# Single-row products of zeros ahead of 22 slabs of a two-block transformer kernel, and one clearing of banks moved ahead of a slab

## Chip, cores and metric

The kernel runs on one core of a Trainium2 chip. The metric is the device time of one execution in microseconds; the time of a version is the median of its runs.

## What is computed

Two blocks on 256 tokens of width 1024, float32 throughout. The first block is a half-weighted feed-forward layer, a mixer (a short convolution and a gated delta rule), a second half-weighted feed-forward layer and a norm. The second block is a mixer of a long convolution and latent attention, and a squared-ReLU MLP. The change touches the two feed-forward layers above all:

```python
def swiglu_ffn(x, w_in, w_out):          # w_in 1024 x 5632, w_out 2816 x 1024
    gate, up = jnp.split(x @ w_in, 2, axis=-1)
    return (jax.nn.silu(gate) * up) @ w_out

h = x
h = h + 0.5 * swiglu_ffn(rmsnorm(h, ffn1_norm), ffn1_w_in, ffn1_w_out)
u = rmsnorm(h, mix_norm) @ w_mix_in      # then the mixer, from 15 column slabs of u
...
h = h + 0.5 * swiglu_ffn(rmsnorm(h, ffn2_norm), ffn2_w_in, ffn2_w_out)
return rmsnorm(h, final_norm)
# second block: z = (norm(h) * (1 + scale) + shift) @ w_in_2, column slabs again
```

## The kernel before

Every weight matrix is cut into slabs of 1 MB (128 partitions x 2048 floats) that pass through three slots. SyncE loads a slab into `raw`. ScalarE rounds it to the high part `wh`. VectorE takes the difference as the low part `wl`. TensorE then makes three products for each pair of 128x128 tiles, high x high, high x low and low x high, so that a slab is 48 pairs of a weight load and a matmul of 256 columns. A slot is free for ScalarE's next cast when TensorE's counter `taken` passes it. Only TensorE's program is changed:

- `wide` (L2006) is a slab of an input projection. It waits for the low part (`low_done`) and writes one bank of the accumulator memory. Its 48 matmuls are all line L2019.
- `deep` (L2055) is a slab of a feed-forward layer's output projection, 48 matmuls on line L2063, added into banks 0 to 3. The MLP of the second block has `deep_rows` (L2075) instead, 24 matmuls of 512 columns on line L2071.
- `clear_sums` (L2084) makes four products of zeros, one row by 512 columns, on line L2087. They zero banks 0 to 3 ahead of the sums of `deep`. The operand `zero` is one partition of 512 bf16 zeros.
- `modulate` (L2107) turns a piece of an unrelated vector, two float32 products of one column on line L2111. The trace shows each of them as two matmuls, so x4.
- `square_sums` (L2115) sums squares for a norm, four float32 products of 256 columns on line L2118. The trace shows x8.
- `ffn` (L2121) runs a feed-forward layer: a first gate slab, the norm's sums, a first up slab, then a hardware loop of 10 passes. A pass is a wait for the gate bank to be read, the next gate slab, a wait for the up bank, the next up slab, a wait for the low part of the hidden values, one `deep` slab, and `modulate`. The last output slab (L2167) stands behind the loop. In `ffn1` the banks are cleared ahead of the first up slab and four transposes (L2144) stand behind it; in `ffn2` the clearing stands behind the up slab, as the last thing ahead of the loop.
- `mix(n)` (L2203) is slab n of the mixer's input projection; slab 0 is followed by `square_sums("n2")`, and slabs 1 to 5 follow in one piece.
- In the second block the slabs of `glu` (eight, in four pairs), `lat` (three) and `gate_b` 0 follow each other (L2388 on). The first half of each glu pair goes to one bank and the second to another. GpSimd's long convolution (lines L766 to L781) starts when the first pair is evacuated.

TensorE's order is the order of its program. A wait in it holds everything behind.

Of the kernel before, what the change touches and what calls it, by code (L numbers as in the profile page):

```python
# [16 lines left out]
P = 128  # L17
# [263 lines left out]
def two_blocks(nc, a):  # L281
    with ExitStack() as ctx:
# [5 lines left out]
        def sb(name, shape, dt=F32, where=ctx):  # L288
            if name in HOMES:
                fill = (HOMES[name] - next_byte[0]) % TURN  # L290
                if fill:
                    next_byte[0] += fill
                    where.enter_context(nc.sbuf_tensor("before_" + name, [P, fill // 4], F32))
            next_byte[0] += math.prod(shape[1:]) * (2 if dt == BF16 else 4)
            return where.enter_context(nc.sbuf_tensor(name, shape, dt))
# [17 lines left out]
        zero = sb("zero", [1, 512], BF16)  # L313
# [23 lines left out]
        ps = [ctx.enter_context(nc.psum_tensor(f"ps{i}", [P, 512], F32)) for i in range(8)]  # L337
# [135 lines left out]
        def S(name):  # L473

            name = SHARED.get(name, (name, 0))[0]
            if name not in named:
                named[name] = sem("s_" + name)
            return named[name]

        def at(name, count):  # L480

            return S(name), count + SHARED.get(name, (name, 0))[1]
# [1522 lines left out]
        def _(pe):  # L2005
            def wide(s, bank, x, y, tile_ready=None, tile_base=0, slab=None, m_tiles=2, inputs=range(KT),  # L2006
                     by_tile=False, low_ready=None):

                slab = s if slab is None else slab
                pe.wait_ge(*(low_ready or (low_done, s + 1)))  # L2010
                n = KT * P * m_tiles
                h, l = (w[:, slab % SLOTS, 0:n].rearrange("p (k m) -> p k m", k=KT) for w in (wh, wl))
                order = [(m, k) for k in inputs for m in range(m_tiles)] if by_tile else \
                    [(m, k) for m in range(m_tiles) for k in inputs]
                for m, k in order:
                    if tile_ready is not None and m == 0:
                        pe.wait_ge(*at(tile_ready, tile_base(k)))
                    for j, (w, r) in enumerate(((h, x), (h, y), (l, x))):
                        mm = pe.matmul(bank[:, m * T:(m + 1) * T], w[:, k, m * P:(m + 1) * P], r[:, k, :],  # L2019
                                       start=(m == 0 and k == 0 and j == 0), stop=(k == KT - 1 and j == 2),  # L2020
                                       skip_group_check=True)
                if inputs[-1] == KT - 1:
                    mm.then_inc(taken, 1)
# [60 lines left out]
            def clear_sums():  # L2084

                for b in range(4):
                    pe.matmul(ps[b][:, :], zero[0:1, 0:P], zero[0:1, :], start=True, stop=True, skip_group_check=True)  # L2087

            def column_sums(n, src, k_tiles, out, ready, signal=True, by_pair=False):
                pe.wait_ge(*at(*ready))  # L2090
                for k in range(k_tiles):
                    if by_pair and k % 2 == 0 and k:
                        pe.wait_ge(*at(ready[0], ready[1] + k // 2))
                    mm = pe.matmul(out, ones, src(k), start=(k == 0), stop=(k == k_tiles - 1), skip_group_check=True)
                if signal:
                    mm.then_inc(S(n + "_stat"), 1)
# [18 lines left out]
            def square_sums(n):  # L2115
                for b in range(4):
                    pe.wait_ge(*at(n + "_add", b + 1))
                    mm = pe.matmul(ps[6][:, 0:T], ones, sq[:, 2 * b, :], start=(b == 0), stop=(b == 3), skip_group_check=True)  # L2118
                mm.then_inc(S(n + "_stat"), 1)

            def ffn(name, n, high, low, prev_free):  # L2121
                s0 = FIRST[name + "_gate"]
                gate_bank, up_bank = (ps[b] for b in FF_BANKS[name])
                if name == "ffn1":
                    first_slab(gate_bank)
                else:
                    wide(s0, gate_bank, high, low, n + "_xl", one, by_tile=True)
                if name == "ffn1":
                    for k in range(KT):
                        if k % 2 == 0:  # L2130
                            pe.wait_ge(*(at("n1_sq", k // 2 + 1) if k < 4 else at("n1_sq_last", k // 2 - 1)))
                        mm = pe.matmul(ps[6][:, 0:T], ones, sq[:, k, :], start=(k == 0), stop=(k == KT - 1), skip_group_check=True)
                    mm.then_inc(S("n1_stat"), 1)
                    pe.wait_ge(*at("x_in", 4))
                    clear_sums()
                    wide(s0 + 1, up_bank, high, low)
                else:
                    square_sums(n)
                if name == "ffn1":
                    pe.wait_ge(*at("n1_std", 1))  # L2140
                    pe.wait_ge(*at("vec_loaded", 16 * (N_VEC - 1)))
                    for g in range(4):
                        rows_g = STAGE_ROWS[g]
                        mm = pe.transpose(ps[6][:, g * P:g * P + rows_g], stage[0:rows_g, g, :], ident[0:rows_g, 0:rows_g])  # L2144
                    mm.then_inc(S("vec_turned"), 1)
                if prev_free:
                    pe.wait_ge(*at(*prev_free))
                if name == "ffn2":
                    wide(s0 + 1, up_bank, high, low)
                    clear_sums()  # L2150
                with pe.Fori(0, FF_STEPS - 1) as i:
                    s = s0 + 2
                    pe.wait_ge(*at(name + "_gate", i + 1))
                    wide(i * 3 + s, gate_bank, high, low, slab=s)
                    pe.wait_ge(*at(name + "_up", i + 1))
                    wide(i * 3 + (s + 1), up_bank, high, low, slab=s + 1)
                    pe.wait_ge(*at(name + "_fl", i + 1))
                    deep(i * 3 + (s + 2), slab=s + 2)
                    modulate(i + (0 if name == "ffn1" else FF_STEPS - 1))
                pe.wait_ge(*at(name + "_fl", FF_STEPS))  # L2160
                s = s0 + 3 * FF_STEPS - 1
                pe.wait_ge(low_done, s + 1)
                h, l = (w[:, s % SLOTS, :].rearrange("p (k m) -> p k m", k=2) for w in (wh, wl))
                for m in range(KT):
                    for k in range(2):
                        for w, r in ((h, last_high[name]), (h, last_low[name]), (l, last_high[name])):
                            mm = pe.matmul(ps[m // 2][:, (m % 2) * T:(m % 2 + 1) * T], w[:, k, m * P:(m + 1) * P], r[:, k, :],  # L2167
                                           start=False, stop=False, skip_group_check=True)
                    if m in (1, 3, 5):
                        mm.then_inc(S(name + "_bank"), 1)  # L2170
                mm.then_inc(taken, 1)
# [35 lines left out]

            mix(0, tile_ready="n2_xl", tile_base=one, by_tile=True)
            square_sums("n2")
            for n in range(1, 6):  # L2210
                mix(n)

# [115 lines left out]
            for h in range(HEADS):  # L2328
                mm = pe.matmul(unit(ps[1], h), unit(k_be, h), unit(tt_mat, HEADS + h), start=(h == 0), stop=True,
                               skip_group_check=True)  # L2330
# [11 lines left out]
            for h in range(HEADS):  # L2342
                pe.matmul(unit(ps[1], h), unit(tt_mat, HEADS + h), unit(v_beta, HEADS + h), start=(h == 0), stop=False,
                          skip_group_check=True)
# [4 lines left out]
            for h in range(HEADS):  # L2349
                pe.matmul(unit(ps[2], h), unit(state, h), q_n[:, h, CH:2 * CH], start=(h == 0), stop=False, skip_group_check=True)  # L2350
                mm = pe.matmul(unit(ps[2], h), unit(v_new, HEADS + h), unit(at_mat, HEADS + h), start=False, stop=True,
                               skip_group_check=True)
# [35 lines left out]
            for n in range(4):  # L2388
                s = FIRST["glu"] + 2 * n
                if n >= 2:  # L2390
                    pe.wait_ge(*at("glu", n - 1))
                wide(s, ps[4 + 2 * (n % 2)], xh, xl, "h_xl" if n == 0 else None, one, by_tile=(n == 0))
                if n == 1:
                    pe.wait_ge(*at("f_kept", 1))
                wide(s + 1, ps[5 + 2 * (n % 2)], xh, xl)
# [22 lines left out]
            for n in range(3):  # L2418
# [5 lines left out]
                for m in range(4):  # L2424
                    for k in range(3):
                        if n == 0 and m == 0:
                            pe.wait_ge(*at("lat_yl", k + 1))
                        for j, (w, r) in enumerate(((h, yh), (h, yl), (l, yh))):
                            mm = pe.matmul(ps[QUERY_BANKS[n][m // 2]][:, (m % 2) * T:(m % 2 + 1) * T], w[:, k, m * P:(m + 1) * P],  # L2429
                                           r[:, k, :], start=(m % 2 == 0 and k == 0 and j == 0), stop=(k == 2 and j == 2),  # L2430
                                           skip_group_check=True)
# [8 lines left out]
            for m in range(NH):  # L2440
                for k in range(2):
                    for j, (w, r) in enumerate(((h, yh), (h, yl), (l, yh))):
                        mm = pe.matmul(ps[KEY_BANKS[m // 2]][:, (m % 2) * T:(m % 2 + 1) * T], w[:, k, m * P:(m + 1) * P],
                                       r[:, 3 + k, :], start=(m % 2 == 0 and k == 0 and j == 0), stop=(k == 1 and j == 2),
                                       skip_group_check=True)
# [8 lines left out]
            for b, bank in enumerate(VALUE_BANKS):  # L2454
# [3 lines left out]
                for k in range(2):  # L2458
                    for j, (w, r) in enumerate(((h, yh), (h, yl), (l, yh))):
                        mm = pe.matmul(ps[bank][:, :], r[:, 3 + k, tk * P:(tk + 1) * P], w[:, k, half * 512:(half + 1) * 512],  # L2460
                                       start=(k == 0 and j == 0), stop=(k == 1 and j == 2), skip_group_check=True)
# [42 lines left out]
            for h in range(NH):  # L2504
# [3 lines left out]
                if h % 2 == 0:  # L2508
                    n = h // 4 + 1
# [98 lines left out]
            for k in range(ADA_MLP * SLOTS + 1, MLP_STEPS):  # L2608
# [3 lines left out]
                if k == MLP_STEPS - 1:  # L2612
                    pe.wait_ge(*at("gate_ready", 1))
                    for t in range(KT):
                        mm = pe.matmul(ps[5 + t // 4][:, (t % 4) * P:(t % 4 + 1) * P], mods[:, 3, t:t + 1].to_broadcast([P, P]), ident,
                                       start=(t % 4 == 0), stop=True, skip_group_check=True)
# [3 lines left out]
                    for tk in range(2):  # L2620
                        mm = pe.matmul(ps[7][:, T + tk:T + tk + 1], z_eps[:, tk * P:(tk + 1) * P], ones[:, 0:1], start=(tk == 0),
                                       stop=True, skip_group_check=True)
# [33 lines left out]
```

## Time and profile before

| | |
|---|---|
| runs | 1014.54, 1014.75, 1016.36 us; median 1014.75 |
| profiled execution | 1016.84 us, with a span of 1015.0 us from first to last instruction |
| TensorE busy | 994.7 us, 98% of the span, 7777 matmuls |
| VectorE, ScalarE, GpSimd busy | 795.4, 502.6, 505.8 us |
| mean granted TensorE clock | 0.994 |
| matmuls of L2019 | 5,064 of 7,777 |

A matmul's row has a modelled duration that overlaps its neighbours, so what a slab costs is read from the distance between starts, or from the pieces of the chain that ended last: a piece runs from the end of what stood before it to its own last end, and 48 matmuls of 256 columns in one piece divide into a spacing.

### The profile page before, as it was taken

To read this page: it belongs to the slowest core of one execution; us is meant where nothing else is said; L and a number is where in the kernel's file an instruction comes from. 1 tells how busy PE (TensorE), PEld (TensorE's weight loads), DVE (VectorE), ACT (ScalarE), POOL (GpSimd) and SP (SyncE) were. 2 spreads that over 40 slices of the span, in tenths; PEclk is the share of its full clock that TensorE was granted. 3 is DMA by queue.
4 is the path that set the end of the run, shared out by engine and by line. 5 is a ranking of instruction groups with operands and counts; after the bars stand their busy time and mean duration, and the time that the engine had idled before them with its cause. 6 is when DMAs were issued, how large, how long until landed. Compare 5 with 4: busy or idle time off the path is not lost.

```text
span 1015.0 us, 19068 instructions
## 1 busy us (share of the span) xinstructions
PE 994.7 (98%) x7777; PEld 950.4 (94%) x7777; DVE 795.4 (78%) x801; ACT 502.6 (50%) x590; POOL 505.8 (50%) x294
## 2 busy tenths in 40 slices
PE   9999999999999999999999999999989999999997
PEld 7999999998999999999999999988979979999986
DVE  5877777699985579878777869998978887778764
ACT  7443433477532464444343766667657463434432
POOL 4676757510043017557677789998950104224400
PEclk9999999999999999999999999999989999999999
DMA  8968677646340266677677366482226627676641
GB/s 269 333 211 277 215 261 235 214 135 192 90 160 1 83 209 213 215 263 233 231 256 247 89 214 179 113 248 84 84 83 199 191 68 249 209 243 209 209 164 42
DMA packets 165997, 188.33 MB, mean 186 GB/s; under 512 B 10574, under 2 KB 155548, under 8 KB 165820
## 3 DMA queue, kind: packets, MB, share of 16 engines
q1 hardware_dynamic: 165580, 186.13, 56.9%
q0 software_dynamic: 192, 1.36, 0.4%
q8 instruction: 35, 0.57, 0.2%
q10 hardware_dynamic: 176, 0.15, 0.1%
q14 instruction: 14, 0.11, 0.0%
HBM read 186.58 MB, written 1.05 MB: 185 GB/s over the span
## 4 chain that ended last, share of the span: by engine, by line
PE 79%; DVE 11%; POOL 4%; ACT 3%; issue 2%; DMA 0%; ACTq 0%; DVEq 0%; POOLq 0%
PE ps L2019 47%; PE ps L2063 11%; PE ps L2071 9%; DVE wl L1304 3%; PE ps L2296 2%; POOL work L781 2%; DVE ps L1696 2%; POOL con L778 2%; PE ps L2242 2%; PE ps L2167 1%; ACT wh L812 1%; PE ps L2111 1%; POOL work L774 1%; PE ps L2429 1%; PE ps L2460 1%
## 5 line engine op out<-in xcount | busy, mean ns | idle before, releaser
L2019 PE MATMUL ps<-xh,wh 128*128 128x256 f32 x1208 | 341.1, 282 | 3.5 <-DVE xl L1653 1.0
L2019 PE MATMUL ps<-xl,wh 128*128 128x256 f32 x1208 | 336.8, 279 | 0.0
L2019 PE MATMUL ps<-xh,wl 128*128 128x256 f32 x1208 | 336.8, 279 | 0.0
L1309 DVE TENSOR_TENSOR wl<-raw,wh 128x2048 fp32r<-128x2048 f32 x78 | 245.6, 3149 | 59.6 <-ACT wh L818 59.6
L2019 PEld LDWEIGHTS ps<-xh,wh 128*128 128x128 f32 x1208 | 227.7, 189 | 7.8 <-issue 5.1
L2019 PEld LDWEIGHTS ps<-xl,wh 128*128 128x128 f32 x1208 | 228.0, 189 | 0.5
L2019 PEld LDWEIGHTS ps<-xh,wl 128*128 128x128 f32 x1208 | 227.4, 188 | 0.0
L818 ACT ACTIVATE wh<-raw 128x2048 fp32r<-128x2048 f32 x78 | 149.4, 1917 | 136.8 <-PE ps L2019 136.8
L1304 DVE TENSOR_TENSOR wl<-raw,wh 128x2048 fp32r<-128x2048 f32 (+1 forms) x72 | 178.5, 2486 | 33.2 <-ACT wh L812 32.5
L672 POOL TENSOR_TENSOR ada_raw<-ada_raw,c_act 128x2048 f32<-128x2048 f32 x24 | 90.1, 3755 | 206.4 <-DMA ada_raw<-in_w_ada 201.3
L812 ACT ACTIVATE wh<-raw 128x2048 fp32r<-128x2048 f32 (+1 forms) x74 | 139.3, 1887 | 60.4 <-PE ps L2019 45.9
L2019 PE MATMUL ps<-yh,wh 128*128 128x256 f32 x480 | 136.9, 285 | 1.2 <-DVE work L1824 0.7
L2019 PE MATMUL ps<-yl,wh 128*128 128x256 f32 x480 | 134.9, 281 | 0.0
L2019 PE MATMUL ps<-yh,wl 128*128 128x256 f32 x480 | 134.8, 281 | 0.0
L675 POOL TENSOR_TENSOR ada_raw<-ada_raw 128x1024 f32<-128x1024 f32 x24 | 97.6, 4069 | 1.9
L2019 PEld LDWEIGHTS ps<-yh,wh 128*128 128x128 f32 x480 | 90.9, 189 | 2.7 <-DVE work L1824 1.4
L2019 PEld LDWEIGHTS ps<-yl,wh 128*128 128x128 f32 x480 | 91.7, 191 | 0.1
L2019 PEld LDWEIGHTS ps<-yh,wl 128*128 128x128 f32 x480 | 91.4, 190 | 0.0
L2063 PE MATMUL ps<-fh,wh 128*128 128x256 f32 x320 | 89.8, 280 | 0.0
L2063 PE MATMUL ps<-fl,wh 128*128 128x256 f32 x320 | 89.8, 280 | 0.0
L2063 PE MATMUL ps<-fh,wl 128*128 128x256 f32 x320 | 89.8, 280 | 0.0
L705 POOL TENSOR_TENSOR work<-work 128x256 f32<-128x256 f32 x13 | 12.9, 995 | 126.8 <-ACT work L835 68.5
(415 smaller groups left out, 1847.6 us busy)
## 6 DMA issues: line engine op xcount, KB each, us to landing
raw<-in_ffn_w_in SPq DMA_DIRECT2D x43, 1024.0 KB, 7.3
ada_raw<-in_w_ada SPq DMA_DIRECT2D x24, 1024.0 KB, 5.0
raw<-in_ffn_w_out SPq DMA_DIRECT2D x22, 1024.0 KB, 4.9
raw<-in_w_in SPq DMA_DIRECT2D x18, 1024.0 KB, 5.4
raw<-in_w_mlp_in SPq DMA_DIRECT2D x16, 1024.0 KB, 5.6
raw<-in_w_mlp_out SPq DMA_DIRECT2D x16, 1024.0 KB, 4.9
raw<-in_w_mix_in SPq DMA_DIRECT2D x14, 1024.0 KB, 5.3
raw<-in_w_mix_out SPq DMA_DIRECT2D x4, 1024.0 KB, 5.1
```

The lines of the kernel that those rows point to most:

```text
L672: pool.tensor_tensor(ada_raw[:, :, :], ada_raw[:, :, :], c_act[:, :].unsqueeze(2).to_broadcast([P, KT, 256]), ALU.mult).then_inc(S("ada_pa ...
L675: pool.tensor_tensor(flat[:, 0:1024], flat[:, 0:1024], flat[:, 1024:2048], ALU.add).then_inc(S("ada_part"), 1)
L778: ins = pool.tensor_scalar(tap_own[:, n, :], upad[:, t, k:k + T], tap(k, t), 0.0, ALU.mult, ALU.add)
L781: ins = pool.tensor_tensor(sums, sums, tap_own, ALU.add)
L812: act.activation(wh[:, s % SLOTS, 0:n], raw[:, s % SLOTS, 0:n], ACT.Copy).then_inc(high_done, 1)
L818: act.activation(wh[:, s % SLOTS, :], raw[:, s % SLOTS, :], ACT.Copy).then_inc(high_done, 1)
L1304: dve.tensor_tensor(wl[:, s % SLOTS, 0:n], raw[:, s % SLOTS, 0:n], wh[:, s % SLOTS, 0:n].bitcast(F32), ALU.subtract).then_inc(low_done, 1)
L1309: dve.tensor_tensor(wl[:, s % SLOTS, :], raw[:, s % SLOTS, :], wh[:, s % SLOTS, :].bitcast(F32), ALU.subtract).then_inc(low_done, 1)
L1696: ins = dve.scalar_tensor_tensor(dst, upad[:, t, k:k + T], tap(k, t), conv_sum(t), ALU.mult, ALU.add)
L2019: mm = pe.matmul(bank[:, m * T:(m + 1) * T], w[:, k, m * P:(m + 1) * P], r[:, k, :], start=(m == 0 and k == 0 and j == 0), stop=(k == KT - ...
L2063: mm = pe.matmul(ps[m // 2][:, (m % 2) * T:(m % 2 + 1) * T], w[:, k, m * P:(m + 1) * P], r[:, k, :], start=False, stop=False, skip_group_c ...
L2071: mm = pe.matmul(ps[n][:, :], r[:, k, tk * P:(tk + 1) * P], w[:, k, half * 512:(half + 1) * 512], start=False, stop=stop, skip_group_check ...
```

## The change

It adds a helper, `long_zeros(bank)`, which makes one product of zeros, one row by 512 columns, into a whole bank. It is called in four places: in every pass of both feed-forward loops ahead of the gate slab, behind the wait for the gate bank and into that bank (20 executions); once ahead of the mixer's slabs 1 to 5 (into bank 5); and once between the first and the second slab of `glu` (into bank 5). In each case the slab that follows starts its own sum in that bank, so the zeros are overwritten. In `ffn2` the four clearing products move from behind the first up slab to ahead of it.

```diff
+            def long_zeros(bank):
+
+                pe.matmul(bank[:, :], zero[0:1, 0:P], zero[0:1, :], start=True, stop=True, skip_group_check=True)
+
...
                 if name == "ffn2":
+                    clear_sums()
                     wide(s0 + 1, up_bank, high, low)
-                    clear_sums()
                 with pe.Fori(0, FF_STEPS - 1) as i:
                     s = s0 + 2
                     pe.wait_ge(*at(name + "_gate", i + 1))
+                    long_zeros(gate_bank)
                     wide(i * 3 + s, gate_bank, high, low, slab=s)
                     pe.wait_ge(*at(name + "_up", i + 1))
                     wide(i * 3 + (s + 1), up_bank, high, low, slab=s + 1)
...
             mix(0, tile_ready="n2_xl", tile_base=one, by_tile=True)
             square_sums("n2")
+            long_zeros(ps[5])
             for n in range(1, 6):
                 mix(n)
...
                 wide(s, ps[4 + 2 * (n % 2)], xh, xl, "h_xl" if n == 0 else None, one, by_tile=(n == 0))
+                if n == 0:
+                    long_zeros(ps[5])
                 if n == 1:
                     pe.wait_ge(*at("f_kept", 1))
                 wide(s + 1, ps[5 + 2 * (n % 2)], xh, xl)
```

On TensorE, at the start of `ffn2`, the program before has the norm's sums (into bank 6), then the first up slab (into bank 4):

```order
L2019 MATMUL ps5<-yh,wl 128x256
L2118 MATMUL ps6<-work1,con 128x256 x4
L2019 MATMUL ps4<-yh,wh 128x256
L2019 MATMUL ps4<-yl,wh 128x256
L2019 MATMUL ps4<-yh,wl 128x256
```

and behind that slab the four clearing products, the loop's entry and the first gate slab of the loop (into bank 5):

```order
L2019 MATMUL ps4<-yh,wl 128x256
L2087 MATMUL ps0<-zero 128x512
L2087 MATMUL ps1<-zero 128x512
L2087 MATMUL ps2<-zero 128x512
L2087 MATMUL ps3<-zero 128x512
L2151 UNCONDITIONAL_BRANCH
L2151 ISA
L2010 ISA
L2019 MATMUL ps5<-yh,wh 128x256
L2019 MATMUL ps5<-yl,wh 128x256
```

In the changed program the same place reads, with its lines numbered four or five higher, the norm's sums, the clearing products and then the up slab:

```order
L2019 MATMUL ps5<-yh,wl 128x256
L2122 MATMUL ps6<-work1,con 128x256 x4
L2087 MATMUL ps0<-zero 128x512
L2087 MATMUL ps1<-zero 128x512
L2087 MATMUL ps2<-zero 128x512
L2087 MATMUL ps3<-zero 128x512
L2019 MATMUL ps4<-yh,wh 128x256
L2019 MATMUL ps4<-yl,wh 128x256
```

and behind the up slab the loop's entry, with the new product as the first matmul of the pass:

```order
L2019 MATMUL ps4<-yh,wl 128x256
L2155 UNCONDITIONAL_BRANCH
L2155 ISA
L2091 MATMUL ps5<-zero 128x512
L2010 ISA
L2019 MATMUL ps5<-yh,wh 128x256
L2019 MATMUL ps5<-yl,wh 128x256
```

So the four clearing products have moved past one slab, and a single one has taken their place in front of the first gate slab. From the second pass on, the new product has the four matmuls of `modulate` (into bank 7) in front of it. Nothing moves on the other engines.

## Rows read from the trace of the kernel before

**Rows 1.** The page: busy time, and the granted clock in 40 slices

```profile
PE 994.7 (98%) x7777; PEld 950.4 (94%) x7777; DVE 795.4 (78%) x801; ACT 502.6 (50%) x590; POOL 505.8 (50%) x294
...
PEclk9999999999999999999999999999989999999999
```

**Rows 2.** Chain that ended last, ffn1: start us, us, what

```profile
20.19 0.96 PE ps L2087 x4
21.15 5.66 PE ps L2019 x48
...
27.20 10.89 PE ps L2019 x96
38.09 5.44 PE ps L2063 x48
43.53 0.34 PE ps L2111 x4
43.87 11.41 PE ps L2019 x96
55.29 5.65 PE ps L2063 x48
```

**Rows 3.** The same chain at the start of ffn2

```profile
379.89 5.65 PE ps L2019 x48
385.55 0.96 PE ps L2087 x4
386.51 11.10 PE ps L2019 x96
397.61 5.44 PE ps L2063 x48
...
403.39 11.42 PE ps L2019 x96
414.81 5.65 PE ps L2063 x48
```

**Rows 4.** The same chain: mixer slabs 1 to 5, start of glu

```profile
213.67 28.28 PE ps L2019 x240
...
572.88 34.27 PE ps L2019 x288
```

**Rows 5.** The same chain elsewhere: behind L2218, and in the MLP

```profile
325.88 1.82 PE ps L2218 x8
327.70 5.85 PE ps L2019 x48
...
868.17 0.34 PE ps L2111 x4
868.51 5.57 PE ps L2019 x48
```

**Rows 6.** Timeline of TensorE, ffn1: start us, us, engine, line, what

```profile
43.37 0.50 PE L2111 MATMUL ps<-con,ada_sum 128*128 128x1 f32 x4
43.73 0.36 PE L2019 MATMUL ps<-xh,wh 128*128 128x256 f32 x1
43.94 0.28 PE L2019 MATMUL ps<-xl,wh 128*128 128x256 f32 x1
```

**Rows 7.** Timeline of TensorE around the four clearing products of ffn2

```profile
385.27 0.28 PE L2019 MATMUL ps<-yh,wl 128*128 128x256 f32 x1
385.48 1.03 PE L2087 MATMUL ps<-zero 1*128 1x512 bf16 x4
386.44 0.39 PE L2019 MATMUL ps<-yh,wh 128*128 128x256 f32 x1
386.66 0.28 PE L2019 MATMUL ps<-yl,wh 128*128 128x256 f32 x1
```

**Rows 8.** Stretches: us, busy us of each engine (instructions), clock, DMA share

```profile
43.40:200.00 156.60, 156.60 (x1334) 156.60 (x1333) 116.72 (x64) 61.92 (x46) 108.65 (x36) 1.00 0.73 241
213.70:241.90 28.20, 28.20 (x241) 28.07 (x241) 27.03 (x39) 19.67 (x25) 0.00 (x0) 1.00 0.66 188
577.40:640.80 63.40, 63.40 (x540) 63.40 (x540) 51.48 (x57) 40.74 (x51) 53.15 (x42) 1.00 0.60 174
641.00:664.00 23.00, 21.81 (x181) 21.29 (x179) 22.79 (x22) 15.18 (x24) 21.88 (x19) 1.00 0.52 128
```

**Rows 9.** Waits of GpSimd, then TensorE: total us, times, longest

```profile
POOL work L766 <- DVE work L1709: 7.0, 1, 7.0
POOL work L774 <- ACT hid L1053: 2.3, 1, 2.3
...
PE ps L2540 <- DVE work L1813: 2.7, 1, 2.7
```

## The prediction

> **What bounds the kernel now.** I read the page first. TensorE is busy 98% of the span and the clock is at full speed, 2.4 GHz, in nearly every slice [rows 1]. In the loop passes behind the first of `ffn1` TensorE is busy all of 156.6 us, while VectorE has 116.72, ScalarE 61.92 and GpSimd 108.65 [rows 8]. TensorE's own waits are few and lie elsewhere, the longest being 2.7 us at L2540 [rows 9]. So in the loops a nanosecond put in front of TensorE costs one and a nanosecond taken out gains one, as long as the others keep up.
>
> Then I read the chain of waits, because it lets one divide. The same 48 matmuls of `deep` take 5.44 us in the first pass of `ffn1` and 5.65 in the second [rows 2]: 113.3 ns from start to start, against 117.7. In `ffn2` it is the same, 5.44 in the first pass and 5.65 in the second [rows 3]. Shape, clock and operands are alike. The two input slabs of a pass show it too: 10.89 and 11.10 us in first passes, 11.41 and 11.42 in the next [rows 2, 3]. So there are two spacings, 4.4 ns apart, and a stream keeps the one it has: 240 matmuls of the mixer take 28.28 us (117.8 ns) and the first 288 of `glu` 34.27 (119.0 with the entry) with no change in between [rows 4].
>
> What stands ahead tells which. The wide spacing begins behind the L2111 products [rows 2, 3]. The narrow one is there behind the four clearing products, in both feed-forward layers. In `ffn2` the slab just ahead of the clearing ran at the wide one (5.65 us for 48) and the slab behind it at the narrow one. This is the reading on which my forecast rests: a 512-column product of zeros puts the stream that follows into the narrow spacing, and L2111 puts it back. What in the array makes the difference no row shows.
>
> **The change, part by part.**
>
> The new product itself. The trace has no single one, only four in a row. In steady state each adds 0.22 us. The entry and the exit cost more: from the last matmul ahead (385.27) to the second behind (386.66) are 1.39 us [rows 7]. Less three further products (0.65) and the two ordinary steps (0.24), one product in the middle of a slab stream would cost 0.50. Behind L2111 it is cheaper, since an entry is paid there already. The last zero product starts its successor 0.07 us ahead of its modelled end (386.51 against 386.44), and the zeros start 0.07 us ahead of the end of what stands before (385.55 against 385.48) [rows 7]. L2111 ends at 43.87 [rows 6], so a zero product would start near 43.80 and, by the distance from the last zero to the next matmul (0.30), the gate slab near 44.10 instead of 43.73. In pieces of the chain, which go from end to end, the zero product adds 0.31 us. Bounds: 0.24, if it can start right behind the last of the four small matmuls, and 0.50, the price in mid-stream. I take 0.31.
>
> The Trainium skill (TensorE: Matmul & The Clock Gate, "Back-to-back issue gap") gives one gap for a warm matmul, N/2.4 + 2.5 ns, which is 109 ns for 256 columns. The trace shows 113.3 and 117.7 instead. By that rule the spacing depends on columns alone and no product ahead could shorten it; the sum would then be only the cost of the new products, which is the time of the second rival below.
>
> A pass, from the second on. Behind a zero product the two input slabs take 11.10 us, as behind the clearing of `ffn2`, instead of 11.42, and `deep` 5.44 instead of 5.65 [rows 3]. That is 0.53 less, against 0.31 more: 0.22 gained a pass. Nine such passes in each layer make 18, so 4.0 us (with the bounds of the product's price, 0.5 to 5.2). The last output slab (L2167) stands behind L2111 with no zeros ahead of it and stays wide.
>
> The first passes. In `ffn1` the stream behind the transposes is narrow already, so the product only costs: 0.31, and 0.21 more because an entry behind zeros is longer (11.10 against 10.89) [rows 2, 3]: 0.5 lost. In `ffn2` the clearing moves ahead of the up slab. A slab behind a clearing takes 5.66 us [rows 2] and the one behind the norm's sums now 5.65 [rows 3]: the narrow spacing only pays for the entry. The clearing costs 0.96 on either side, and the new product then adds 0.31. So 0.3 lost.
>
> The mixer. The product costs 0.31. Slabs 1 to 5 then take 5.66 and four times 5.44, 27.42 us instead of 28.28 [rows 2, 4]: 0.55 gained on TensorE. VectorE is busy 27.03 of 28.20 us in this stretch [rows 8], so it has 1.2 us in hand over five slabs, and I book 0.45 (bounds 0.1 and 0.55).
>
> `glu`. The product stands between two slabs that follow without a gap: 0.31. The eleven slabs behind the first then take 5.66 + 10 x 5.44 = 60.06 us instead of 11 x 5.65 = 62.15, so TensorE would be 1.8 us ahead at about 640.8. Will it arrive at the end? Against it: from 641 to 664 VectorE is busy 22.79 of 23.00 us [rows 8], and GpSimd's long convolution starts only when VectorE has evacuated the first pair of slabs (it waits 7.0 us for L1709, then has one later wait of 2.3 for a scaled tap) [rows 9]. The first pair comes 0.31 later and gains only about 0.2 in its second slab, so that start does not move forward. For it: VectorE is busy only 51.48 of 63.40 us up to 640.8 [rows 8] and can follow TensorE, and GpSimd's 2.3 us wait is for ScalarE, which would come earlier. Bounds: 0.3 lost (convolution a little later, nothing else arrives) and 1.8 gained. I take half, 0.9 gained.
>
> Sum: -4.0 + 0.5 + 0.3 - 0.45 - 0.9 = -4.55 us. The profiled execution, 1016.84 us with a span of 1015.0, becomes 1012.3 with a span near 1010.5; that execution is 2.1 us over the median, which I carry over, so the forecast is 1014.75 - 4.6 = 1010.2. Nothing here is hidden under other work; if VectorE's cover in the mixer and after `glu` is gone, those two terms fall away and 1011.6 stands. With the end values of all terms the narrow-everywhere case runs from 1007.9 (-5.2 + 0.4 + 0.2 - 0.55 - 1.8) to 1015.7 (-0.5 + 0.7 + 0.5 - 0.1 + 0.3), and 1008.2 to 1012.5 holds most of it.
>
> **The rivals.**
>
> *Half of it (12%).* One product may not do what four do, or only in some passes. For: L2218, eight float32 matmuls in 1.82 us, left the slab behind it at 5.85, wide with a long entry [rows 5], so a longish interruption does not always reset the stream; and in the MLP a slab right behind the same L2111 products takes 5.57 us, narrow with an entry [rows 5], so what stands ahead of L2111 counts too. The state has more inputs than I can name. If 9 of 18 passes turn narrow: -9 x 0.22 + 9 x 0.31 = +0.8, the first passes +0.8, mixer and `glu` -1.35: +0.25, near 1015.0.
>
> *No narrow spacing at all (12%), slower.* One mechanism: a single product is too short to move the stream, and its price is paid every time on an engine with no slack. 18 x 0.31 = 5.6, first passes +0.8, mixer and `glu` +0.6: +7.0, near 1021.8. It decides when fewer than about nine passes turn. For: no row shows a lone product, and the skill's rule has only one gap. Against: each of the clearings in the two layers is followed by narrow matmuls, behind transposes and slabs alike [rows 2, 3], and what is next to the stream is the last zero product, the same one way or the other.
>
> *More than that (6%).* The narrow state survives L2111 where the pass before was narrow, so that L2167 and the mixer's slab 0 are narrow as well, and all of `glu`'s 1.8 arrives: 1008.5 or below. Against: the first pass of each layer was narrow and L2111 ended it [rows 2, 3].
>
> **How the numbers follow.** Narrow everywhere has 70%, at 1010.2; about 0.2% (2 us) is what a measurement of this kernel can tell. It is faster by more than that in 65 of its 70, and the largest rival adds 6. The half case falls within 0.2% for the most part (10 of 12), the rest beyond on the slow side; with the 5 of 70, "same" has 15. The slower rival has 12 and 2 from the half case. The range from 1007.0 to 1016.5 holds the first case nearly whole, most of the half case and part of the largest; it leaves out the slower rival. The likeliest case's own range is 1008.2 to 1012.5.
>
> **What the new profile would show.** One L2091 row ahead of each gate slab. Right: `deep` pieces of 5.44 in every pass, pairs of input slabs near 11.10, a pass of about 17.2 us instead of 17.4; the mixer's 240 matmuls near 27.4; no new TensorE waits in the loops. Wrong: `deep` at 5.65 behind a lone product, or at 5.44 only in alternate passes; a zero product that costs 0.5 or more; waits of TensorE for `wl` in the mixer; the time gained by 640.8 given back at L2429 or L2540.

## The result, and the profile after

The changed kernel takes 1020.25 us (median of 10 runs, 1017.99 to 1023.3) against 1015.91 us for the kernel before on the same chip (10 runs, 1014.53 to 1019.62). The ratio is 1.0039, with a 95% interval of 1.0025 to 1.0053: slower by 0.4%, where I had forecast 0.45% faster. The profiled execution took 1019.87 us with a span of 1018.1, 3.1 us more than before.

The page first, with the row that answers to [rows 1]: TensorE's busy time and share, then the other engines.

```profile
PE 996.0 (98%) x7799; PEld 945.4 (93%) x7799; DVE 804.8 (79%) x801; ACT 503.3 (49%) x590; POOL 506.0 (50%) x294
...
PEclk9999999999999999999999999999989999999999
```

The 22 new products are there, the clock is as it was, and TensorE still has 98% of the span: its busy time grew by 1.3 us, the span by 3.1. Where the time went has to be read from the chain. In the new line numbers the product of zeros is L2091, `modulate` L2115, `square_sums` L2122 and the last output slab L2172. The chain that ended last, in `ffn1` (start us, us, what), beside [rows 2]:

```profile
20.18 0.96 PE ps L2087 x4
21.14 5.66 PE ps L2019 x48
26.80 0.39 PE ps L2148 x4
27.19 0.32 PE ps L2091
27.51 11.10 PE ps L2019 x96
38.61 5.44 PE ps L2063 x48
44.05 0.34 PE ps L2115 x4
44.38 0.32 PE ps L2091
44.70 11.10 PE ps L2019 x96
...
61.90 11.10 PE ps L2019 x96
```

Up to here all is as forecast. A pass is 17.19 us (from 27.51 to 44.70, and to 61.90), against 17.41 before, in all ten passes. The product costs 0.31 to 0.32. The mixer, beside [rows 4]:

```profile
212.27 0.32 PE ps L2091
212.59 27.45 PE ps L2019 x240
```

27.45 us for the five slabs, where 27.42 was forecast and 28.28 stood before. The start of `ffn2`, beside [rows 3]:

```profile
376.09 1.73 PE ps L2122 x8
377.82 0.96 PE ps L2087 x4
378.79 5.66 PE ps L2019 x48
384.44 0.32 PE ps L2091
384.76 11.51 PE ps L2019 x96
396.26 5.65 PE ps L2063 x48
401.92 0.34 PE ps L2115 x4
402.25 0.32 PE ps L2091
402.57 11.50 PE ps L2019 x96
```

Here it goes wrong. The up slab behind the clearing is narrow, 5.66 as costed. Behind the lone product come 11.51 and 5.65, the wide spacing, and it stays for all ten passes. A pass is now 17.81 us: 0.40 more than before and 0.62 more than the 17.19 that I had put in. The timeline of TensorE shows the entry (start us, modelled us):

```profile
384.05 0.28 PE L2019 MATMUL ps<-yl,wh 128*128 128x256 f32 x1
384.16 0.28 PE L2019 MATMUL ps<-yh,wl 128*128 128x256 f32 x1
384.37 0.39 PE L2091 MATMUL ps<-zero 1*128 1x512 bf16 x1
384.69 0.39 PE L2019 MATMUL ps<-yh,wh 128*128 128x256 f32 x1
384.91 0.28 PE L2019 MATMUL ps<-yl,wh 128*128 128x256 f32 x1
385.03 0.28 PE L2019 MATMUL ps<-yh,wl 128*128 128x256 f32 x1
...
385.97 0.28 PE L2019 MATMUL ps<-yl,wh 128*128 128x256 f32 x1
```

From 385.03 to 385.97 are eight steps of 117.5 ns. Ahead of the product the steps were 0.11 us.

Then `glu`, beside the second line of [rows 4], and the first 288 matmuls after the long convolution:

```profile
575.38 6.07 PE ps L2019 x48
581.46 0.32 PE ps L2091
581.77 27.43 PE ps L2019 x240
...
772.57 34.87 PE ps L2019 x288
```

The `glu` slabs behind the product are narrow in this execution; the slab ahead of it was wide (its last four steps take 0.47 us, 580.71 to 581.18). The piece at 772.57 is 1.10 us longer than its counterpart before (33.77 at 770.39), and nothing was changed near it.

Put side by side, the starts of the same pieces give the account of the 3.1 us, after less before: mixer slabs 1 to 5, 212.59 against 213.67, -1.08; the last twelve matmuls ahead of the norm's sums of `ffn2`, 374.41 against 376.53, -2.12; first input slabs of its loop, 384.76 against 386.51, -1.75; start of `glu`, 575.38 against 572.88, +2.50; the piece behind the long convolution, 772.57 against 770.39, +2.18; its end +3.3; the last instruction +3.1. So `ffn2`'s passes alone lose 4.25 us. That is the first pass, 0.62 longer since it was narrow before, and nine times 0.40.

### The profile page after: what moved, and what is told of

It reads as the page before. It is cut to its first block, busy times and chain, and to the rows that moved or that the text cites. A ratio compares the mean times of both kernels' runs of the same rounds, so it can differ in the third digit from the quotient of the medians.

```text
span 1018.1 us, 19111 instructions
## 1 busy us (share of the span) xinstructions
PE 996.0 (98%) x7799; PEld 945.4 (93%) x7799; DVE 804.8 (79%) x801; ACT 503.3 (49%) x590; POOL 506.0 (50%) x294
## 3 DMA queue, kind: packets, MB, share of 16 engines
HBM read 186.58 MB, written 1.05 MB: 184 GB/s over the span
## 4 chain that ended last, share of the span: by engine, by line
PE 80%; DVE 11%; POOL 4%; issue 2%; ACT 2%; DMA 0%; ACTq 0%; DVEq 0%; POOLq 0%
PE ps L2019 47%; PE ps L2063 11%; PE ps L2071 9%; DVE wl L1304 3%; PE ps L2302 2%; POOL work L781 2%; DVE ps L1696 2%; POOL con L778 2%; PE ps L2248 2%; PE ps L2172 1%; ACT wh L812 1%; PE ps L2115 1%; PE ps L2091 1%; POOL work L774 1%; PE ps L2030 1%
## 5 line engine op out<-in xcount | busy, mean ns | idle before, releaser
L675 POOL TENSOR_TENSOR ada_raw<-ada_raw 128x1024 f32<-128x1024 f32 x24 | 87.9, 3664 | 1.9
```

What stands on the lines that cost most here:

```text
L675: pool.tensor_tensor(flat[:, 0:1024], flat[:, 0:1024], flat[:, 1024:2048], ALU.add).then_inc(S("ada_part"), 1)
```

## The experiments

The narrow spacing was there behind a lone product in `ffn1` and not in `ffn2`. My theory on reading this ("history"): a lone product doesn't set the spacing, it changes it according to what stands directly ahead. In `ffn1` four transposes stand between the up slab and the first product, in `ffn2` a narrow slab does. The rivals were the accumulator bank (the two layers use banks 4 and 5 crosswise), the buffer slot of the slab, and chance. The ratios below are against the kernel before on the same chip, with 95% intervals. A time without a number of runs is that of a single, profiled execution: what counts there is the spacing, and the time is only a guide.

**The changed kernel once more.** No edit.

> The changed kernel once more, to see whether the spacing of each place is a property of the program or of the execution. Place theory (something in the program of ffn2, bank, slot or operand, makes a lone zero product fail there): all ten passes of ffn1 narrow again (deep 5.44 us), all ten of ffn2 wide again (5.65 us, input slabs 11.50). Chance theory: in another execution the passes of ffn2 come out narrow, or those of ffn1 wide, and the time moves by up to 5 us.

1020.59 us. All ten passes of `ffn1` are narrow again and all ten of `ffn2` wide, so this is no chance. `glu` differs from the first execution. Its chain:

```profile
574.28 6.03 PE ps L2019 x48
580.32 0.32 PE ps L2091
580.63 28.48 PE ps L2019 x240
```

Wide, 1.05 us more than 27.43. The slab ahead was narrow here (its last three steps take 0.34 us, 579.70 to 580.04), the same picture as in `ffn2`, and the reverse of the first execution's `glu`. The other profiles agree. Of twelve executions with one product there (these two and ten of the versions below), the slab ahead was wide in six, and the stream behind the product narrow; in the other six it was the other way round. So the spacing of the first slab changes from one execution to the next, and the product exchanged it every time.

**Banks exchanged.**

```diff
-FF_BANKS = {"ffn1": (4, 5), "ffn2": (5, 4)}
+FF_BANKS = {"ffn1": (5, 4), "ffn2": (4, 5)}
```

> The changed kernel with the gate and up banks exchanged in both layers: ffn1 now has its gate slab and zero product in bank 5, ffn2 in bank 4. Bank theory (a lone zero product into bank 5 leaves the stream wide in a loop): ffn1 turns wide (deep 5.65 us) and ffn2 narrow (5.44 us), ffn1 about 5 us longer and ffn2 about 6 us shorter. Slot or operand theory: nothing moves, ffn1 5.44 and ffn2 5.65.

1021.06 us, and no spacing moves: `ffn1` narrow, `ffn2` wide (11.50 and 5.65 from 385.40 on). The bank theory falls.

**Every slab one slot on.** In all places alike:

```diff
-                h, l = (w[:, slab % SLOTS, 0:n].rearrange("p (k m) -> p k m", k=KT) for w in (wh, wl))
+                h, l = (w[:, (slab + SHIFT) % SLOTS, 0:n].rearrange("p (k m) -> p k m", k=KT) for w in (wh, wl))
```

> The changed kernel with every slab one slot further in memory: the gate slab of ffn1 lies in slot 0 instead of 2, that of ffn2 in slot 1 instead of 0. Slot theory (weights in slot 0 behind a lone zero product go wide): ffn1 turns wide (deep 5.65 us), ffn2 narrow (5.44 us). Bank or operand theory: nothing moves.

1020.52 us, again with `ffn1` narrow and `ffn2` wide. The slot theory falls too.

**No part of the change in `ffn2`.** The clearing stands behind the up slab and the loop has no product; the rest of the change stays.

```diff
-                    clear_sums()
                     wide(s0 + 1, up_bank, high, low)
+                    clear_sums()
...
-                    long_zeros(gate_bank)
+                    if name == "ffn1":
+                        long_zeros(gate_bank)
```

> The changed kernel with ffn2 as in the kernel before: no zero product in its loop, clearing behind the up slab. The zeros of ffn1, the mixer and glu stay. Theory that the loss is in ffn2 alone: ffn2 is back to 17.41 us a pass (its first narrow), and against the kernel before 9 x 0.21 - 0.5 in ffn1 and 0.5 to 1 in the mixer remain, about 2 us faster than the kernel before, near 1014, if the second block does not change. Rival (the second block loses by itself, since its long stretch of 252 matmuls came out wide in the changed kernel): within 1 us of the kernel before.

1014.59 us (10 runs) against 1016.09; ratio 0.9991, interval 0.9976 to 1.0006. `ffn2` is as before, a first pass of 11.10 and 5.44 and then 11.41 and 5.65. Against the change whole (1.0039) this is 0.5% better, so the loss is in `ffn2`, as the account says. The gain of 2 us that I expected to be left is not shown: the interval includes 1, and the rival, a second block that loses by itself, isn't excluded. In this execution both of its long stretches were wide (28.48 us for `glu` behind the product, 34.88 for the 288 matmuls).

**Only the clearing put back, zeros kept in every pass.**

```diff
-                    clear_sums()
                     wide(s0 + 1, up_bank, high, low)
+                    clear_sums()
```

> The changed kernel with one part undone: in ffn2 the four clearing products stand behind the up slab again, so the loop's first zero product has them, and no narrow slab, right ahead of it. History theory (what stands ahead of the first pass sets the spacing, a lone product right behind a narrow slab turns the stream wide, and the pair L2111 plus zero product hands the state of one pass to the next): all ten passes of ffn2 are narrow, deep 5.44 us and input slabs 11.10, a pass 17.19 us instead of 17.81; ffn2 6.2 us shorter than in the changed kernel, the time near 1013.5, 2 us faster than the kernel before. Layer theory (something in ffn2, its operands or its place, makes lone products fail there): the passes stay at 17.81 us and the time near 1020.

1014.84 us (10 runs) against 1017.04; ratio 0.9977, interval 0.996 to 0.9994. The chain at the start of `ffn2`:

```profile
382.78 0.96 PE ps L2087 x4
383.74 0.22 PE ps L2091
383.96 11.09 PE ps L2019 x96
395.05 5.44 PE ps L2063 x48
...
401.15 11.10 PE ps L2019 x96
```

All ten passes narrow, 17.19 us each. The loop is that of the changed kernel; only four products in front of it were moved. Its first product now ends a row of five, and the slab ahead of that row is wide (117.7 ns) as in the kernel before. So the passes of `ffn2` carry what the loop's entry gave them, through nine further lone products and through `modulate`. The price of the move is 0.62 us ten times over. I had costed it at nothing.

**A narrow slab directly ahead of `ffn1`'s first product.** The transposes go ahead of the clearing and the up slab, so that they no longer stand between that slab and the loop.

```diff
+                if name == "ffn1":
+                    clear_sums()
+                    wide(s0 + 1, up_bank, high, low)
```

> The changed kernel with the four transposes and clearing of ffn1 in another order: transposes, clearing, up slab, loop. So the narrow up slab stands right ahead of the loop's first zero product, as in ffn2. History theory: now ffn1 is wide in all ten passes (deep 5.65 us, a pass 17.81) and ffn2 stays as it is, about 6 us slower than the changed kernel. Layer theory: ffn1 stays narrow (5.44 us).

1035.13 us. About 8 us of it is a loss at the start that has nothing to do with the question: the transposes now wait 6.8 us for a load, the up slab behind them takes 7.75 us at a granted clock of 0.73 (from 28 to 36 us), and the loop starts at 36.01 instead of 27.51. The last 14 steps of that slab are narrow, 113 ns. The loop itself answers the question:

```profile
35.69 0.32 PE ps L2091
36.01 11.51 PE ps L2019 x96
47.52 5.65 PE ps L2063 x48
```

`ffn1`, narrow in every version seen up to here with zeros, is now wide in all ten passes. What stands directly ahead of the first product decides for either layer.

**A lone product ahead of every slab of the mixer's five and of `glu`.** `long_zeros` goes into `mix` and into both halves of the pairs.

> The changed kernel with a zero product ahead of each of the mixer's slabs 1 to 5 and of each of the seven glu slabs behind the first, instead of one. Flip theory (a lone product right behind a stream exchanges the spacing): slabs alternate, about 5.65 and 5.44 us for 48 matmuls without the entry, from slab to slab. Reset theory (it gives narrow behind wide and wide behind narrow only by its timing there, or always one of them): all slabs behind a product look the same after the second. Time beyond the changed kernel: 10 x 0.5 = 5 us at most.

1024.41 us. The chain in the mixer:

```profile
212.53 5.67 PE ps L2019 x48
...
218.52 5.85 PE ps L2019 x48
...
224.69 5.66 PE ps L2019 x48
...
230.66 5.85 PE ps L2019 x48
...
236.83 5.67 PE ps L2019 x48
```

With its entry, a slab is 5.66 us narrow and 5.85 wide. They alternate strictly, here and through the seven `glu` slabs behind a product (5.85, 5.66, 5.85, 5.66, 5.85, 5.66, 5.87). Directly behind a slab, then, a lone product exchanges the spacing: narrow becomes wide, and wide narrow. Had I had this row, the forecast for `ffn2` would have been wide.

**Two, three and four products a pass.** The same call written two, three or four times ahead of the gate slab. A new question arose from the last run: if one exchanges, do two leave it alone (parity), or does a longer row set the narrow one (reset)?

> The changed kernel with two zero products in each pass of both loops instead of one. Flip theory (parity counts): behind the narrow slab of ffn2 two products leave it narrow, and ffn2 comes out other than now in at least its first pass. Length theory (a row of products resets to narrow, a lone one does not): all passes of both layers narrow, 17.19 + 0.22 = 17.41 us a pass. If both fail, ffn2 stays wide at 18.03 us a pass.

1022.43 us. Passes alternate in both layers; `ffn2`:

```profile
388.49 0.53 PE ps L2091 x2
389.02 11.08 PE ps L2019 x96
400.11 5.44 PE ps L2063 x48
...
406.42 11.50 PE ps L2019 x96
417.92 5.65 PE ps L2063 x48
```

Two directly behind the narrow up slab leave it narrow (11.08), as two exchanges would. Two behind `modulate` exchange: narrow, wide, narrow, wide. One behind `modulate` hands on what it finds, narrow in `ffn1` and wide in `ffn2` above. `modulate` alone left wide behind either (the passes of the kernel before). I have no count that fits all three.

> The changed kernel with three zero products in each pass. With one, a pass hands on its spacing; with two, passes alternated. Parity theory (each zero product exchanges the spacing once, L2111 once more): three act as one, ffn1 narrow in all passes from the second on, or all wide, no alternation, about 17.62 or 18.24 us a pass. Reset theory (the row becomes long enough): all passes of both layers narrow.

1020.47 us, all 20 passes narrow; `ffn2`'s first behind the narrow up slab is 11.09 us. Parity wants this one wide. Directly behind a slab it holds for one and two and fails at three.

> The changed kernel with four zero products in each pass, as many as the clearing has. Parity theory: four act as two, the passes alternate between 11.08 and 11.50 us for the input slabs. Reset theory, which the three clearings seen so far suggest (narrow behind them each time, behind a wide slab as behind a narrow one): all twenty passes narrow, 17.84 us each.

1024.75 us, all 20 passes narrow (11.10, then 11.09, and 5.44). A row of three or four ends narrow wherever it was tried. But in these runs the stream ahead was always narrow. That a longer row also turns a wide stream narrow is seen only at the entry of `ffn2`: four in [rows 3] and again in the version without zeros there, five in the one with the clearing back. For three it wasn't tried. It doesn't pay: a pass is 17.61 us with three and 17.83 with four, against 17.41 with none.

**The product behind `modulate`, and four in `glu`.** With the clearing back, the lone product becomes the last matmul of the pass, so that it also stands ahead of L2172.

```diff
-                    long_zeros(gate_bank)
...
                     modulate(i + (0 if name == "ffn1" else FF_STEPS - 1))
+                    long_zeros(ps[6])
...
-                    long_zeros(ps[5])
+                    for _ in range(4):
+                        long_zeros(ps[5])
```

> A version meant to be faster: clearing of ffn2 back behind its up slab, the loop's lone zero product as the last matmul of a pass (behind L2111, into bank 6) instead of the first, and four zero products instead of one between the first two slabs of glu. Then the first passes pay for no product and the last output slab stands behind one. If the handing-on rule holds: all twenty passes narrow at 17.19 us, L2167 narrow (5.65 becomes 5.44 with a longer entry), 0.3 to 0.5 us a layer less than with the product in front; glu narrow for 11 slabs whatever its first slab was, 0.65 dearer. Against clearing_back: 0 to 1 us faster. Rival: the product's new place breaks the handing-on and the passes come out wide, then near 1020.

1014.98 us (11 runs) against 1017.41; ratio 0.9977, interval 0.9964 to 0.999. L2172 is narrow with an entry (5.66, against 5.76), all passes are narrow, and so is `glu` behind its four products (27.43, the slab ahead narrow too). It is not faster than the version with the clearing back (1014.27 beside it, below), where I had expected up to 1 us. The reset by four, though, is no rule. In this execution `ffn1`'s up slab came out wide behind its clearing, which has the norm's sums ahead of it and no slab:

```profile
18.78 0.96 PE ps L2087 x4
19.74 5.86 PE ps L2019 x48
```

The two slabs behind the four transposes were narrow all the same (10.90 us), as they are in [rows 2] behind a narrow slab. So, as far as these traces go, the transposes end narrow behind either, and the loop of `ffn1` was entered narrow.

**The version with the clearing back, once more.** No new edit, for its interval.

> clearing_back once more beside zeros_behind_modulate, for its time on the same chip and to see whether its spacings repeat: all passes narrow again, 2 us faster than the kernel before.

1014.27 us (11 runs) against 1017.41; ratio 0.9978, interval 0.9964 to 0.9991. All 20 feed-forward passes are narrow again. The 288 matmuls behind the long convolution took 34.88 us here and 33.76 in the first execution of the same kernel, so that stretch changes by itself. The two versions with the clearing back have the lowest ratios, 0.22 to 0.23% ahead of the kernel before; the version without zeros in `ffn2` (0.9991) overlaps with them.

## Why the prediction was wrong

**Price of one product: right.** 0.31 forecast, 0.31 to 0.32 measured as a piece of the chain behind `modulate`, behind L2122 and between two slabs. Between two slabs the longer entry of the next one comes on top (5.66 against 5.44), so the whole price there is about 0.5: from the last matmul ahead (384.16) to the second behind (384.91) are 0.75 us, less two ordinary steps 0.51. The 0.50 worked out for mid-stream was right too.

**`ffn1` and the mixer: right.** The nine passes gained 0.22 each and the first lost 0.5, as worked out. The mixer came to 27.45 against 27.42, and its lead arrived: -1.08 at the start of its slabs, of which the product had taken 0.31, and -1.93 at 255.65 (257.58 before). Twelve matmuls ahead of the sums of `ffn2` the changed kernel led by 2.12 us; the terms booked up to there add to 1.95.

**The failed step: "a 512-column product of zeros puts the stream that follows into the narrow spacing, and L2111 puts it back".** Every clearing that I had read was four products in a row, and I put one in. The experiments show what stands in its place. One product exchanges the spacing when it stands directly behind a slab. `modulate` alone makes the next pass wide; with one product it hands the spacing on, with two it exchanges it, and with three or four a narrow stream stayed narrow. That is why `ffn1` came out right for a wrong reason, by luck: its loop was entered narrow behind the transposes, and one product behind `modulate` hands on what it finds.

**"The clearing costs 0.96 on either side": the sum was right, the side effect missed.** The move took away the four products that made the entry narrow, and left a narrow slab directly ahead of a lone one. Forecast for the passes of `ffn2` behind that entry, -2.0; measured +4.25. This is 6.2 of the 7.6 us between the span that was forecast for the profiled execution (1010.5) and the measured one (1018.1). The other 1.4 is mostly the stretch at 772.57 (1.1) and `glu` (0.6, below).

**`glu`: the product exchanges there too, and what it finds changes.** Narrow behind it (27.43) in one execution, wide (28.48) in the next. The forecast took the first slab to be wide, as in the one trace I had; it was so in six of twelve. Where the slabs behind were narrow, little arrived in the changed kernel: the lag fell from 2.50 to 2.18 us, a gain of 0.3 for the 0.9 booked. That is inside the bounds of 0.3 lost and 1.8 gained. In the first execution with the clearing back 1.4 arrived (from -4.33 at 568.55 to -5.68 at 764.71). Over all profiles, from the start of `glu` to the piece behind the long convolution are 197.51 us before, 196.15 to 197.65 in the six executions with the one product that were narrow behind it, and 197.48 to 199.89 in the five that were wide. So, against the one trace of before, the product mostly gains in the first case and mostly loses in the second, and the 0.9 could not be booked. It isn't the spacing alone: with four products it took 200.17, and the slabs were narrow.

**The rivals.** "Half of it" had the mechanism nearest to the truth, "one product may not do what four do", and even the count: ten passes narrow, ten wide. I put it at 1015.0, and 12 in 100, since I charged a wide pass 0.31. It costs 0.40, because a wide entry behind a product is 11.50 instead of 11.42, and there are ten of them in a row, the first of which had been narrow. "No narrow spacing at all", 1021.8, is close to the measured time by accident: its mechanism is refuted by `ffn1`. The formula that I had weighed (the Trainium skill, TensorE: Matmul & The Clock Gate, "Back-to-back issue gap") is given there for an isolated matmul. For streams of weight loads and matmuls the same section has one measured spacing for 128 columns and one for 512, and none for 256. I should have said so. Neither knows a second spacing at one number of columns, and the traces have two, 113.3 and 117.7 ns by the pieces of 5.44 and 5.65.

**A slip in the sum.** The lower end of the narrow-everywhere case is 1007.8 by its own terms, not 1007.9; nothing hangs on it.

**What stays open.** What in TensorE keeps and exchanges the spacing; no row shows it. Also open is why three products do not exchange where one does, and why four did not set the narrow spacing once. Bank and slot are ruled out; whether it is the number of products or the length of the interruption that counts was not tried apart. With all passes narrow, the forecast of 0.45% should have come nearly whole, yet three such measurements give 0.22 to 0.23%, with intervals from 0.06 to 0.40%. The traces show two places where a part of it went. One is `glu`, whose 0.9 us can't be counted on. The other is the end of `ffn1`'s loop: in the two executions with the clearing back the last passes take up to 17.45 us instead of 17.19, 0.4 us in all in the first and 0.15 in the second, and what held them was not looked into. From the start of `ffn1`'s loop to the start of `glu` these executions gain 3.27 and 3.05 us on the one trace of the kernel before, where the terms up to there add to 3.75. The streams of the second block vary by 1.1 us by themselves besides; whether they vary more often to the slow side in the new kernels was not measured.

## What to carry to other kernels

When a short instruction seems to put a stream into a better rhythm, count how many of them stood there and what stood on both sides, and reproduce both; a row of four is no evidence for one. A state that a loop hands from pass to pass is decided at its entry, so an edit ahead of a loop that costs nothing in place can be worth its effect times all passes. Two edits that each gain, or cost nothing, are to be timed together and apart: here the zeros alone gave 0.9977 and the zeros with the moved clearing 1.0039.

## What the runs showed of the hardware

- A stream of weight loads and 256-column matmuls has two spacings, 113.3 and 117.7 ns, at the same granted clock (1.00 in the stretches of either). It kept the one that it entered with for at least 240 matmuls (27.43 and 28.48 us, the same slabs).
- A single product of one row by 512 columns directly behind such a stream moves it to the other spacing, in both directions, 12 times in 12 (five mixer slabs of which four stand behind a slab, seven of `glu`, and the entry of `ffn2`), and likewise at `glu`'s product in eleven further executions. It costs 0.32 us as a piece of the chain and 0.5 with the longer entry of the next slab.
- Long streams without any such neighbour come out at either spacing in different executions of one kernel (33.76 and 34.88 us). Executions of one kernel differ by 4.6 to 6.4 us where ten or more were taken, and this can be a part of it.
